# Two of four gathered tiles: value rows scaled on ScalarE and summed by accumulating transposes

## What is computed

```
def chunk(xc):                                   # 128 tokens
    q = (xc @ w_q).reshape(128, 8, 2, 128)
    s = einsum('thpd,pnd->thpn', q, sub_keys)
    sv, si = top_k(s, 16)
    ...                                          # 256 candidates, the 16 best: idx
    g = softmax(top_s)
    act = gelu(einsum('td,thkd->thk', xc, u[idx]))
    return einsum('thk,thkd->td', g * act, v[idx])
```

## Time and profile before

| | |
|---|---|
| median of 3 runs | 2372.15 us (2371.76 to 2375.93) |
| span of the profiled execution | 2643.4 us |
| time of the profiled execution around its span | not shown for this kernel |
| PE busy | 2537.3 us, 96% of the span |
| DVE, ACT, POOL busy | 1595.0, 1111.4, 702.4 us |
| mean granted TensorE clock | 0.741 |
| moved by DMA | 768.22 MB, mean 291 GB/s |

### The profile page before, as it was taken

The page is one execution under the profiler, slowest core; times in us unless marked ns, Lnnn a source line. Parts: engine busy times, 40 slices in busy tenths (PEclk is TensorE's granted clock), DMA queues, the critical chain, the costliest instruction groups (busy, mean ns, idle before and its releaser), DMA issues.

```text
span 2643.4 us, 28258 instructions
## 1 busy us (share of the span) xinstructions
PE 2537.3 (96%) x9756; PEld 1535.3 (58%) x9756; DVE 1595.0 (60%) x3700; ACT 1111.4 (42%) x2732; POOL 702.4 (27%) x624
## 2 busy tenths in 40 slices
PE   7879999999999999999999999999999999999998
PEld 7758999777999998644333334443334443333432
DVE  4554566656556676856667537536726554677665
ACT  4353433425443333444444436434426443445443
POOL 0000001010001100744555224324423333444443
PEclk7667777777777777777777777777777777777777
DMA  5203467452447754899999999999989997999997
GB/s 208 80 1 126 154 218 284 166 183 88 135 168 252 258 198 134 314 362 396 420 420 420 346 342 378 347 339 413 410 317 344 357 349 289 421 420 420 421 420 309
DMA packets 131348, 768.22 MB, mean 291 GB/s; under 512 B 14480, under 2 KB 16272, under 8 KB 59280
## 3 DMA queue, kind: packets, MB, share of 16 engines
q0 software_dynamic: 87552, 587.24, 56.3%
q1 hardware_dynamic: 42944, 177.81, 19.6%
q10 hardware_dynamic: 720, 1.51, 0.2%
HBM read 765.45 MB, written 1.05 MB: 290 GB/s over the span
## 4 chain that ended last, share of the span: by engine, by line
PE 84%; DMA 7%; ACT 4%; DVE 3%; issue 1%; SPq 0%; ACTq 0%; POOL 0%; DVEq 0%
PE bank L904 34%; PE bank L547 11%; PE bank L548 10%; PE bank L549 10%; PE bank L938 8%; DMA arena<-experts,arena 7%; PE bank L679 1%; PE bank L659 1%; PE bank L626 1%; PE bank L647 1%; ACT L1421 1%; DVE arena L2268 1%; PE bank L576 1%; ACT L1431 1%; ACT arena L1240 0%
## 5 line engine op out<-in xcount | busy, mean ns | idle before, releaser
L904 PE MATMUL bank<-arena 128*128 128x512 f32 x2048 | 1204.8, 751 | 26.4 <-ACT arena L1426 24.3
L2268 DVE CUSTOM_DVE_ANT_0 arena<-arena 128x1024 f32<-128x1024 f32 x512 | 636.5, 1245 | 542.3 <-DMA arena<-experts,arena 541.5
L513 POOL DMA_INDIRECT arena<-experts,arena x512 | 617.9, 1207 | 908.7 <-PE bank L904 873.9
L904 PEld LDWEIGHTS bank<-arena 128*128 128x128 f32 x2048 | 411.1, 206 | 759.5 <-issue 599.3
L1166 ACT CAST whi<-wring 128x1024 fp32r<-128x1024 f32 x228 | 238.1, 1048 | 372.4 <-PE bank L549 361.5
L1685 DVE TENSOR_TENSOR wlo<-wring,whi 128x1024 fp32r<-128x1024 f32 x216 | 263.3, 1224 | 207.4 <-ACT whi L1166 207.1
L1421 ACT ACTIVATE arena<-arena 128x1 f32<-128x1 f32 x512 | 102.6, 200 | 441.5 <-DVE arena L2268 439.4
L499 POOL DMA_DIRECT2D arena<-ada_w x64 | 34.0, 532 | 789.5 <-DVE adaM L1732 771.2
L1426 ACT ACTIVATE arena<-tab,arena 128x128 f32<-128x128 f32 x512 | 205.5, 401 | 16.7
L547 PE MATMUL bank<-hTh,whi 128*128 128x256 f32 (+1 forms) x576 | 190.9, 331 | 16.8 <-DVE hTl L1694 9.3
L938 PE MATMUL bank<-wring,hfT 128*128 128x512 f32 x320 | 188.6, 746 | 0.0
(11 more groups left out here) (327 smaller groups left out, 3264.6 us busy)
## 6 DMA issues: line engine op xcount, KB each, us to landing
wring<-w_stream SPq DMA_DIRECT2D x236, 512.0 KB, 3.5
wring<-w_stream SPq DMA_DIRECT2D x48, 1024.0 KB, 6.8
arena<-ada_w POOLq DMA_DIRECT2D x64, 512.0 KB, 4.8
alibi<-ada_w POOLq DMA_DIRECT2D x32, 512.0 KB, 4.7
arena<-experts,arena POOLq DMA_INDIRECT x512, 10.6
xT<-xT_in SPq DMA_DIRECT2D x1, 1088.0 KB, 5.2
alibi<-alibi_in ACTq DMA_DIRECT2D x1, 1024.0 KB, 5.4
tab<-tab_in SPq DMA_DIRECT2D x1, 831.0 KB, 6.6
```

Of the source, the lines that this page charges most:

```text
L513: pool.indirect_dma_start(g_ring[:, r], None, experts[n // (2 * PEER_HEADS)], bass.IndirectOffsetOnAxis(idx[:, s // SLOTS % 2, s % SLOTS:s ...
L904: last = mm(banks[2 * t + b][:, :], diag[:, r], g_ring[:, r, D + b * TILE_N:D + (b + 1) * TILE_N], start=s % SLOTS == 0, stop=s % SLOTS == ...
L2268: v.tensor_tensor_reduce(g_ring[:, r, 0:D], g_ring[:, r, 0:D], hrow[:, t], 1.0, 0.0, ALU.mult, ALU.add, act8[:, r:r + 1]).then_inc(dot_don ...
```

## The change

For gathered tiles 1 and 2 (`TURNED`) ScalarE writes no diagonal. It multiplies the `v` half of the buffer, 128 x 1024, by the coefficients in place, and counts the same `diag_ready`. TensorE then adds the scaled rows by eight transposes of 128 x 128 that accumulate in the same two banks; the accumulator holds a feature in a partition. With that, the copy to `frow` and the eight transposes after tiles 1 and 2 (q = 2 and q = 4) go away, and VectorE's `norm_parts` reads the accumulator, after a wait for the last slot of the tile on `slot_used`. Tile 0 and tile 3 keep the diagonals. No DMA is added or taken away.

```diff
+TURNED = (1, 2)
...
+        gather_of = {0: 0, 2: 1, 4: 2}
+        by_rows = [q for q in range(5) if gather_of.get(q) not in TURNED]
...
             def slot(s):
...
-                for b in range(2):
-                    last = mm(banks[2 * t + b][:, :], diag[:, r], g_ring[:, r, D + b * TILE_N:D + (b + 1) * TILE_N],
-                              start=s % SLOTS == 0, stop=s % SLOTS == SLOTS - 1)
+                first, final = s % SLOTS == 0, s % SLOTS == SLOTS - 1
+                if s // SLOTS in TURNED:
+                    for c in range(KC):
+                        last = mm(banks[2 * t + c // 4][:, (c % 4) * P:(c % 4 + 1) * P], g_ring[:, r, D + c * P:D + (c + 1) * P],
+                                  ident, start=first and c % 4 == 0, stop=final and c % 4 == 3, is_transpose=True)
+                else:
+                    for b in range(2):
+                        last = mm(banks[2 * t + b][:, :], diag[:, r], g_ring[:, r, D + b * TILE_N:D + (b + 1) * TILE_N],
+                                  start=first, stop=final)
...
             def norm_parts(q):      # TensorE
-                pe.wait_ge(f_copied, 2 * q + 2)
-                turn_8(4, lambda c: frow[:, c * P:(c + 1) * P], ft_done)
+                if q in by_rows:
+                    pe.wait_ge(f_copied, 2 * by_rows.index(q) + 2)
+                    turn_8(4, lambda c: frow[:, c * P:(c + 1) * P], ft_done)
...
             def gelu(s):            # ScalarE
-                af(diag[:, r], ident, ACT.Copy, scale=coef8[:, r:r + 1]).then_inc(diag_ready, 1)
+                if s // SLOTS in TURNED:
+                    af(g_ring[:, r, D:2 * D], g_ring[:, r, D:2 * D], ACT.Copy, scale=coef8[:, r:r + 1]).then_inc(diag_ready, 1)
+                else:
+                    af(diag[:, r], ident, ACT.Copy, scale=coef8[:, r:r + 1]).then_inc(diag_ready, 1)
...
-            def copy_f(t, q):
-                n = q // 2 if q < 4 else q - 2
-                act.wait_ge(slot_used[RING - 1], (n + 1) * (SLOTS // RING))
+            def copy_f(q):
+                if q not in by_rows:
+                    return
+                act.wait_ge(slot_used[RING - 1], (gather_of[q] + 1) * (SLOTS // RING))
...
             def norm_parts(q):      # VectorE
+                if q in by_rows:
+                    b0 = 4
+                else:
+                    b0 = 2 * t
+                    dve.wait_ge(slot_used[RING - 1], (gather_of[q] + 1) * (SLOTS // RING))
                 for c in range(KC):
-                    dve.wait_ge(ft_done, 2 * q + c // 4 + 1)
-                    last = v.scalar_tensor_tensor(xnt[:, c], banks[4 + c // 4][:, (c % 4) * P:(c % 4 + 1) * P],
+                    if q in by_rows:
+                        dve.wait_ge(ft_done, 2 * by_rows.index(q) + c // 4 + 1)
+                    last = v.scalar_tensor_tensor(xnt[:, c], banks[b0 + c // 4][:, (c % 4) * P:(c % 4 + 1) * P],
```

More of the change, by code:

```diff
@@ L1434, in copy_rows @@
             def copy_rows(b, q):
-                if q:
-                    act.wait_ge(ft_done, 2 * q)
+                if by_rows.index(q):
+                    act.wait_ge(ft_done, 2 * by_rows.index(q))
                 nc.scalar.copy(frow[:, b * TILE_N:(b + 1) * TILE_N], banks[frow_bank[q] + b][:, :]).then_inc(f_copied, 1)
-            def copy_f(t, q):
-                n = q // 2 if q < 4 else q - 2
-                act.wait_ge(slot_used[RING - 1], (n + 1) * (SLOTS // RING))
+            def copy_f(q):
+                if q not in by_rows:
+                    return
+                act.wait_ge(slot_used[RING - 1], (gather_of[q] + 1) * (SLOTS // RING))
                 for b in range(2):
@@ L1473, in mixer_parts @@
                 tile = slice(t * P, (t + 1) * P)
-                copy_f(t, 2 * t)
+                copy_f(2 * t)
                 yield
@@ L1483, in mixer_parts @@
                         act.wait_ge(row_turned, 8 * t + x - 1)
-                    elif x < 2 and t:
-                        act.wait_ge(ft_done, 2 * (2 * t) + 2)
+                    elif x < 2 and t and 2 in by_rows:
+                        act.wait_ge(ft_done, 2 * by_rows.index(2) + 2)
                     copy_row(g0 + x, x, qrow[x % 2] if x < 4 else dv[:, t, (x - 4) * TILE_N:(x - 3) * TILE_N])
@@ L1550, in mixer_parts @@
                     if x < 2:
-                        act.wait_ge(ft_done, 2 * (2 * t + 1) + 2)
+                        act.wait_ge(ft_done, 2 * by_rows.index(2 * t + 1) + 2)
                     else:
@@ L1563, in last_parts @@
             def last_parts(t):
-                copy_f(t, 4 + t)
+                copy_f(4 + t)
                 yield
```

## The result

The changed kernel takes 2379.78 us, median of 11 runs (2372.84 to 2388.15), the kernel before 2372.15 us (2371.34 to 2380.27, 11 runs). The ratio is 1.0025, 95% interval 1.0013 to 1.0036: some 6 us slower, where 38 us less were forecast.

What follows compares the result with a forecast made beforehand. TensorE was taken to bound tiles 1 and 2. They were to go from 815 us to 777 (DMA floor 751 plus 26 for ScalarE), gaining 38: 2372 - 38 = 2334 us, range 2280 to 2400.

Steps and rivals of the forecast that it cites:

- What bounds the kernel: Tiles 1 and 2: TensorE is the bound wherever a part stands beside slots; DMA has 13% and 16% to spare.
- the sum: Whole kernel: profiled span 101 us less; in the runs tiles 1 and 2 go from 815 to 777 us, 38 us gained.
- I take the middle, 815 us: Time of tiles 1 and 2 in the runs before the change, taken between 751 and 878.5 us.
- TensorE per slot: Tiles 1 and 2: eight transposes take 1.2 us a slot instead of 2.27, saving 137 us a tile.
- DMA is what is late next: Tiles 1 and 2: gathers at 420 GB/s set a floor of 751 us; at most 127.5 us of savings show.
- ScalarE per slot: Tiles 1 and 2: scaling takes 0.74 us more a slot; uncovered at the head pairs, costing 0 to 52 us, 26 taken.
- second rival: ScalarE becomes the bound at tiles 1 and 2's head pairs: 26 to 52 us lost, 2398 to 2424 us; chance 0.15.
- The seams: Ends of tiles 1 and 2: copies, transposes and waits go away; counted as nothing, at most 2 x 5 us.
- Hidden anyway: First rival: tiles 1 and 2 already at the DMA floor in the runs, ScalarE covered, time 2372 us; chance 0.13.
- 917 us were left for the tiles: Argument against the first rival: 2372 less 819 (dense stage) and 636 (tiles 0 and 3) leaves 917 for tiles 1 and 2.
- The rule against this: Tiles 1 and 2: the skill says the clock gate doesn't count transposes as PE work, so the clock would be 1.2 GHz.
- third rival: TensorE's clock falls to 0.5 in tiles 1 and 2: 897 us there, 82 us more, 2454 us; chance 0.05.

Runs made afterwards that it cites:

- e1: The kernel before, unchanged, profiled a second time: 2374.92 us, clock 0.964, gathered tiles 1 and 2 together 766.3 us.
- e5: Changed kernel, but ScalarE scales only 128 of 1024 value columns in slots 32 to 59 of tiles 1 and 2, beside the head pairs: 2369.38 us.
- e6: Changed kernel, but in tiles 1 and 2 ScalarE scales 1024 columns only in slots 32 to 59, and 128 in the other 200 slots: 2378.13 us.
- e12: Changed kernel with the change extended to tile 0, so made for tiles 0, 1 and 2: 2377.00 us, ratio 1.0014.
- e4: Kernel before, but in tiles 1 and 2 the second slot matmul is made only for a tile's first and last slot: 2367.15 us, ratio 0.9968.

## Why the prediction was wrong

**What bounds the kernel** was read rightly, but in a profile of another clock. That TensorE had hardly any idle time in tiles 1 and 2 and that DMA had 13 and 16% to spare was true of that execution. In the runs DMA had 1 to 3% to spare (415 and 408 GB/s, e1).

**The step that failed** is the last of the sum, "I take the middle, 815 us". The prediction had seen that TensorE must be faster in the runs and that the two tiles then took between 751 and 878.5 us; they took 766. The bound that left the upper half open was "at full clock the dense stage would still need 819 us". It takes 940 us (e1). The mistake is one of scaling: the stage's 1027 us of TensorE time were multiplied by its mean clock, 0.73, but they only fell to 865, which is 0.84 of them. A part of this is that the stage's clock in e1 is 0.96 and not 1: 1027 x 0.73 / 0.96 = 781 us, 31 more. The other 84 us are work that didn't follow the clock. The dense stage is a chain of short fp32r matmuls, each with its own weight load. Loads and matmuls of one group, ns min/median/max, first in the profile of the prediction, then in e1:

```profile
L547 PEld LDWEIGHTS bank<-mTh,whi x512: 187/222/234, 233.4 to 808.4; 128*128 128x128 f32 x171
L547 PE MATMUL bank<-mTh,whi x512: 276/319/593, 233.5 to 808.6; 128*128 128x272 f32 x86, 128*128 128x256 f32 x85
```

```profile
L547 PEld LDWEIGHTS bank<-mTh,whi x512: 187/188/190, 207.7 to 694.7; 128*128 128x128 f32 x171
L547 PE MATMUL bank<-mTh,whi x512: 276/284/492, 207.8 to 694.8; 128*128 128x272 f32 x86, 128*128 128x256 f32 x85
```

The load takes 188 ns at full clock, 0.85 of its 222 before, and the matmul 284, 0.89 of its 319, where the clock's level went from 0.75 to 1. Neither follows the clock in full; what sets the stage's pace wasn't tried. With 940 us for the dense stage the same subtraction would have left 2372 - 940 - 636 = 796 us for the two tiles, and the middle of 751 and 796 is 773. The other 30 us of the subtraction are in the 636 for tiles 0 and 3: tile 3 with the end was taken at 306 us and takes 334.5, at 398 GB/s (e1).

The rest of the sum would have stood: with 766 us in place of 815 it gives 751 + 26 - 766, 11 us slower, where 6 were measured.

**TensorE per slot**: right. 137 us less a tile was forecast at the profile's clock. In the runs' profiles TensorE's time in a tile goes from 348 to 282 us, with a clock that falls as it idles more. Of that 8 us show.

**DMA is what is late next**: right, and more than said. The floor of 751 us was only 15 us away before the change, and it is 7 us below the best that any relief of TensorE reached (758.3).

**ScalarE per slot**: the mechanism was right (the second rival's, in its mild form), the place too (e5, e6), the size not: 26 us were taken, 11 to 14 measured. A term in it is a misreading of the earlier trace rows: "46 and 47 dots fall there" counts every row of the line, and a dot leaves two, the multiplication and the read of its sum. There were 23 and 24. With 17 and 18 in place of 34 and 35 us more, ScalarE would have needed 68 and 71 us in those 70, just at the limit; in the changed kernel it is at 58 of 60. Against DMA's 63 and 58.5 us the cost without any cover would have been 18 us and not 52, and the measured price is most of that. Taking half of a figure that was too large hid most of the slip.

**The seams**: counted at nothing, and e12, which takes away one more, shows nothing.

**The rivals.** The outcome is the first and the second together. Hidden anyway (0.13) is what happened to TensorE's saving; ScalarE as the bound of the head pairs (0.15) is what was left, at +6 us in place of +26 to 52, since TensorE's relief pays for about half of ScalarE's price. The argument used against the first, that 917 us were left for the tiles, is the one that fell. The time, 2379.78, is in the range of 2280 to 2400, and the sign is wrong.

**The rule against this.** The clock did fall in the two tiles, from 0.96 and 0.98 to 0.82 and 0.81. The third rival asked whether transposes count as work for the clock. e4 has no transposes in its slots, halved matmuls in their place, nearly the same busy time (290 and 283 us) and the same clock, 0.80 and 0.83. The end of tile 1, where slots stand alone, shows it without any other work beside them: all 192 matmul instructions of the changed kernel in this stretch are transposes of L911, all 49 of e4 are slot matmuls. First the changed kernel, then e4:

```profile
1590.00:1650.00 60.00, 39.47 (x192) 32.81 (x192) 42.09 (x106) 45.14 (x81) 32.40 (x25) 0.68 1.01 420
```

```profile
1590.00:1650.00 60.00, 41.58 (x49) 11.13 (x50) 40.59 (x104) 24.64 (x77) 25.33 (x24) 0.68 1.01 420
```

With nothing but transposes the granted clock still goes up to the upper level (2.4 GHz) again and again, to the same mean of 0.68. So for these fp32 transposes the trace does not bear out the rule of the Trainium skill ("TensorE: Matmul & The Clock Gate", Part 4) that the full clock doesn't engage for transpose mode because it isn't counted as PE work in the same way. The clock fell with TensorE's idle time, as it did in e4, and it isn't what lost the time.

## What to carry to other kernels

Before reading which engine bounds a stage, see that the profiled execution is like the runs: when its span is 11% above their median, its bounds need not be theirs. A saving then has to be held against the DMA's floor at the clock of the runs, and stages of short matmuls don't shrink in proportion to the clock. When work moves from the bound engine to one with time to spare, look at that engine in the densest 60 us, not over the tile: here ScalarE had a quarter of each tile free and still cost 11 to 14 us, most of it in one short stretch of each. Count a line's instructions by operation before multiplying.

## What was not expected

Eight accumulating fp32 transposes of 128 x 128 take 1.10 us at the upper clock level, where the four matmul instructions of a slot take 1.98: summing by transposes costs TensorE little more than half. In the one profiled execution that the prediction rests on, the upper level of the granted clock reads 0.75 throughout; in the 13 others that were profiled it reads 1.00. Why stays open.
